# Norm statistics taken by token in thin matmuls, and three reorderings beside them

## The reference

```python
for l in range(2):                                   # first block, 272 tokens
    h = layer_norm(ALPHA*h + 0.5*swiglu(h, w_up1, w_down1))      # norm 0, 3
    h = layer_norm(ALPHA*h + hybrid_mixer(h, ...))               # norm 1, 4
    h = layer_norm(ALPHA*h + 0.5*swiglu(h, w_up2, w_down2))      # norm 2, 5
for l in range(2):                                   # second block, 256 tokens
    x = x + token_mixing(rmsnorm(x), ...)                        # rms 0, 2
    x = x + (swiglu_2, moe_swiglu)[l](rmsnorm(x))                # rms 1, 3
return rmsnorm(x)

def layer_norm(x, g, b): return (x - mean(x)) * rsqrt(mean((x - mean(x))**2) + eps) * g + b
def rmsnorm(x, g):       return x * rsqrt(mean(x*x) + eps) * g
```

## Time and profile before

| | us |
|---|---|
| three runs | 2813.75, 2813.24, 2811.03 |
| median | 2813.24 |
| span of the profiled execution, first to last instruction | 2809.8 |
| PE busy in it | 2745.6 (98%) |

### The profile page before, as it was taken

The page is one execution under the profiler, slowest core; times in us unless marked ns, Lnnn a source line. Parts: engine busy times, 40 slices in busy tenths (PEclk is TensorE's granted clock), DMA queues, the critical chain, the costliest instruction groups (busy, mean ns, idle before and its releaser), DMA issues.

```text
span 2809.8 us, 68032 instructions
## 1 busy us (share of the span) xinstructions
PE 2745.6 (98%) x28028; PEld 2292.6 (82%) x28028; DVE 1982.1 (71%) x1914; ACT 1608.7 (57%) x1723; POOL 700.7 (25%) x562
## 2 busy tenths in 40 slices
PE   9999999999999999999999999999999999999997
PEld 7887788888877888887888887888879788797794
DVE  5457575564576755666855566778899898998986
ACT  5445663354356554455643445657677776777765
POOL 4314022122122221120122011144234243242331
PEclk9999999999999999999999999999999999999999
DMA  9764367576643676553576663469999999999995
GB/s 240 171 199 124 91 194 195 169 191 176 188 134 106 180 206 178 157 181 121 179 189 180 200 187 124 151 240 365 383 386 383 387 387 378 394 383 382 388 384 223
DMA packets 657516, 665.64 MB, mean 237 GB/s; under 512 B 25302, under 2 KB 513116, under 8 KB 657276
## 3 DMA queue, kind: packets, MB, share of 16 engines
q1 hardware_dynamic: 655696, 659.75, 71.5%
q0 software_dynamic: 704, 0.59, 0.4%
q10 hardware_dynamic: 876, 1.79, 0.2%
HBM read 661.01 MB, written 1.05 MB: 236 GB/s over the span
## 4 chain that ended last, share of the span: by engine, by line
PE 91%; DVE 4%; ACT 2%; issue 1%; DVEq 1%; DMA 0%; POOLq 0%; ACTq 0%; SPq 0%; POOL 0%
PE ps L2084 23%; PE ps L2085 23%; PE ps L2086 23%; PE ps L2814 3%; PE ps L2813 3%; PE ps L2812 3%; PE ps L2127 1%; PE ps L2133 1%; PE ps L2128 1%; DVE w_lo L1258 1%; PE ps L2437 1%; PE ps L2417 1%; ACT w_hi L705 1%; PE ps L2747 1%; PE ps L2505 1%
## 5 line engine op out<-in xcount | busy, mean ns | idle before, releaser
L2084 PE MATMUL ps<-x_hi,w_hi 128*128 128x128 f16 (+2 forms) x5440 | 1229.5, 250 | 16.1 <-DVE prod L1273 5.4
L2085 PE MATMUL ps<-x_lo,w_hi 128*128 128x128 f16 (+2 forms) x5440 | 1229.2, 250 | 0.0
L2086 PE MATMUL ps<-x_hi,w_lo 128*128 128x128 f16 (+2 forms) x5440 | 1229.0, 250 | 0.0
L1258 DVE SCALAR_TENSOR_TENSOR w_lo<-w,w_hi 128x2048 f16<-128x2048 f32 (+4 forms) x338 | 692.5, 2059 | 309.4 <-ACT w_hi L705 307.6
L705 ACT ACTIVATE w_hi<-w 128x2048 f16<-128x2048 f32 (+4 forms) x338 | 560.9, 1669 | 83.7 <-PE ps L2086 70.4
L2084 PEld LDWEIGHTS ps<-x_hi,w_hi 128*128 128x128 f16 x5440 | 534.0, 98 | 71.2 <-issue 14.4
L2085 PEld LDWEIGHTS ps<-x_lo,w_hi 128*128 128x128 f16 x5440 | 533.8, 98 | 45.9
L2086 PEld LDWEIGHTS ps<-x_hi,w_lo 128*128 128x128 f16 x5440 | 533.9, 98 | 42.6
L1754 DVE SCALAR_TENSOR_TENSOR w_lo<-w,w_hi 128x2048 f16<-128x2048 f32 x224 | 532.8, 2406 | 40.9 <-ACT w_hi L1178 40.8
L1178 ACT ACTIVATE w_hi<-w 128x2048 f16<-128x2048 f32 x224 | 416.9, 1901 | 28.4 <-DMA w<-in_moe_w_gate 12.0
L2066 POOL CAST ff<-pb 128x512 f16<-128x512 f32 x56 | 137.6, 2458 | 568.5 <-DVE pb L1846 568.5
(11 more groups left out here) (390 smaller groups left out, 4302.3 us busy)
## 6 DMA issues: line engine op xcount, KB each, us to landing
w<-in_ffn_w_up SPq DMA_DIRECT2D x176, 512.0 KB, 5.0
w<-in_moe_w_gate SPq DMA_DIRECT2D x80, 1024.0 KB, 8.1
w<-in_moe_w_up SPq DMA_DIRECT2D x80, 1024.0 KB, 8.7
w<-in_moe_w_down SPq DMA_DIRECT2D x64, 1024.0 KB, 7.8
w<-in_w_in SPq DMA_DIRECT2D x112, 512.0 KB, 4.6
mix<-in_moe_w_down SPq DMA_DIRECT2D x48, 1024.0 KB, 8.0
w<-in_mix_w_in SPq DMA_DIRECT2D x64, 512.0 KB, 4.9
mix<-in_moe_w_gate SPq DMA_DIRECT2D x32, 1024.0 KB, 8.9
```

The costliest lines, as they stand in the source:

```text
L1258: vec.scalar_tensor_tensor(k.w_lo[:, s, 0:size], k.w32[:, s, 0:size], WS, k.w_hi[:, s, 0:size], ALU.mult, ALU.subtract).then_inc(k.parts_r ...
L2084: pe.matmul(acc, w_hi, x_hi, start=first, stop=False)
L2085: pe.matmul(acc, w_hi, x_lo, start=False, stop=False)
L2086: return pe.matmul(acc, w_lo, x_hi, start=False, stop=last)
```

## The change

1. Statistics by token. `windows(t)` cuts the tokens in windows of 128 (three for 272, the last one overlapping, two for 256). `turned_mean` makes the data the stationary operand and one column of `mean_w` the moving one: the result is one column of 128 tokens per window. The root and the reciprocal then work on 128x3 or 128x2 values, and `spread` brings 1/root back to all partitions with one matmul per window (stationary: the column broadcast to 128x128; moving: the identity). DVE's scaling `t` now reads it from PSUM.
2. The sums of the earlier chunks move into the last unit's chain (`within`, behind 8 of its 11 tiles in a down phase, behind 6 of 8 in `wo` and `wout`). The shift by the mean still needs the old wide form (`add_mean`), which stays beside the new one.
3. `keep_warm` becomes 4 idle matmuls ahead of the spread and 8 behind it.
4. The next phase's third unit is split ahead of the norm by ACT and DVE (`over_units_early`, and by hand in `wo` and `wout`). DVE's `up` takes the first product before it splits another unit.
5. ACT squares the latents ahead of `residual`, into `tmp`; the Silu table is loaded inside the norm (`silu=True`); layer 1's vectors are loaded (six DMAs on ACT's queue) ahead of norm 2's phase instead of behind it.

```diff
-KEEP_WARM = 13
+KEEP_WARM, KEEP_WARM_SPREAD = 4, 8
+SUMS_WITHIN, SUMS_WITHIN_WO = 8, 6
...
+def over_units_early(phase, q, split, take):
+    u0 = phase.units - AHEAD - 1
+    for u in range(phase.units):
+        for n in (u + AHEAD,) if u < u0 else (u + AHEAD, u + AHEAD + 1) if u == u0 else (u + AHEAD + 1,):
+            split(phase.first + n, q, phase.size if n < phase.units else UNIT)
+        take(u // SLOTS, u % SLOTS, phase.first + u % SLOTS, q + u // SLOTS)
...
 def layer_norm(n, ...):                                        # ACT
-        act.wait_ge(k.ln_rest, n + 1)
-        act.activation(k.tmp[:, 1, t], k.ps[:, 4, t], ACT.Square).then_inc(k.rest_squared, 1)
-        act.wait_ge(k.ln_spread, n + 1)
-        act.activation(k.std[:, 0, t], k.tmp[:, 1, t], ACT.Sqrt, bias=k.eps[:, 0:1]).then_inc(k.ln_std, 1)
-        split(following + 2, q, UNIT)
+        act.wait_ge(k.ln_var_out, n + 1)
+        act.activation(k.tok_std[:, 0:m], k.tok_var[:, 0:m], ACT.Sqrt, bias=k.eps[:, 0:1]).then_inc(k.ln_std, 1)
+        if silu:
+            act.activation(k.warm[:, :], k.eps[:, 0:1], ACT.Silu)
...
 def wo_norm(n, q):                                             # DVE
         add_pair(2, False)
+        split(g + 5, q, UNIT)
         vec.wait_ge(k.wo_half, n // 3 + 1)
         vec.tensor_tensor(k.h[:, 6, t], k.h[:, 6, t], k.ps[:, 0, t], ALU.add).then_inc(k.wo_half_out, 1)
-        split(g + 5, q, UNIT)
+        split(g + 6, q, UNIT)
...
 def layer_norm(n, g0, b0, last=False):                         # DVE
-        vec.tensor_tensor(k.tmp[:, 1, cols], k.ps[:, 5, cols], k.tmp[:, 1, cols], ALU.subtract).then_inc(k.ln_spread, 1)
-        u(0)
-        vec.wait_ge(k.ln_std, n + 1)
-        vec.reciprocal(k.rstd[:, 0, cols], k.std[:, 0, cols])
+        vec.tensor_tensor(k.tok_var[:, 0:m], k.ps[:, 5, 0:m], k.tok_less[:, 0:m], ALU.add).then_inc(k.ln_var_out, 1)
+        vec.wait_ge(k.ln_std, n + 1)
+        vec.reciprocal(k.tok_rstd[:, 0:m], k.tok_std[:, 0:m]).then_inc(k.ln_inverted, 1)
+        vec.wait_ge(k.ln_rest, n + 1)
+        u(0)
+        vec.wait_ge(k.ln_spread, n + 1)
...
+    def turned_mean(t, x, first=False, last=False, bank=5):    # PE
+        for m, (s, _) in enumerate(windows(t)):
+            a = pe.matmul(k.ps[:, bank, m:m + 1], x[:, s:s + P], k.mean_w[:, 0:1], ...)
+        return a
+    def spread(t, bank=5):
+        for m, (s, row) in enumerate(windows(t)):
+            a = pe.matmul(k.ps[:, bank, s + row:s + P], k.tok_rstd[:, m:m + 1].broadcast_to([P, P]), k.ident[:, row:P], start=True, stop=True)
+        return a
...
+        def within():                                          # down_norm, inside the last chain
+            pe.wait_ge(k.rest_summed, n + 1)
+            add_mean(n, k.prod[:, 1, :], first=True)
+            turned_mean(t, k.prod[:, 1, :], first=True, bank=6)
+            pe.wait_ge(k.squares_summed, n + 1)
+            turned_mean(t, k.prod[:, 0, :], first=True)
...
+                if cut:                                        # wo_norm, second half of unit 3
+                    chain(acc, g % SLOTS, tiles[:cut], k.x_hi[:, :, t], k.x_lo[:, :, t], last=False)
+                    pe.wait_ge(k.squares_summed, n + 1)
+                    turned_mean(t, k.prod[:, 0, :], first=True)
+                    for c in (4, 5):
+                        squared(n, c)
+                        turned_mean(t, k.sq[:, c, :])
+                    squared(n, 6)
+                    turned_mean(t, k.sq[:, 6, :])
+                    pe.wait_ge(k.rest_summed, n + 1)
+                    add_mean(n, k.prod[:, 1, :], first=True)
+                    turned_mean(t, k.prod[:, 1, :], first=True, bank=6)
...
+    def rms_begin(n):                                          # inside wout's and down's last chain
+        pe.wait_ge(k.squares_summed, 3 * DEPTH + n)
+        turned_mean(ALL2, k.prod[:, 0, :], first=True)
```

More of the change, by code:

```diff
@@ L176, with windows @@
 ALL1, ALL2 = slice(0, T1), slice(0, T2)
+def windows(t):
+    starts = [min(c, t.stop - P) for c in range(t.start, t.stop, P)]
+    return [(s, t.start + j * P - s) for j, s in enumerate(starts)]
 def live(l):
@@ L760, in take @@
                 square(n, c)
-        over_units_ahead(act, phase, q, split, take, loop=False)
+        over_units_early(phase, q, split, take)
     def wo_norm(n, l, q, vec0):
@@ L767, in wo_norm @@
         early_squares(n)
+        split(phase.first + phase.units + AHEAD, q, UNIT)
         act.wait_ge(k.vec_evac, vec0 + phase.base + 2 + 3)
@@ L807, in wout_squares @@
         for c in range(KC):
+            if c == 4 and l == 0:
+                split(phase.first + phase.units + AHEAD, 0, UNIT)
             if c == 6:
@@ L2199, in unit @@
                 pe.wait_ge(k.vec_evac, vec0 + (trip * 2 + j // 2) + (phase.base + 1))
-            chain(k.ps[:, 2 * (j // 2), t], g % SLOTS, [(c * P, P, second * half + c) for c in range(half)], a_hi[:, :, t], a_lo[:, :, t],
-                  first=not second, last=bool(second)).then_inc(k.unit_done, 1)
+            acc, s = k.ps[:, 2 * (j // 2), t], g % SLOTS
+            tiles = [(c * P, P, second * half + c) for c in range(half)]
+            if trip * SLOTS + j == 2 * KC - 1:
+                chain(acc, s, tiles[:SUMS_WITHIN], a_hi[:, :, t], a_lo[:, :, t], first=False, last=False)
+                within()
+                tiles = tiles[SUMS_WITHIN:]
+            chain(acc, s, tiles, a_hi[:, :, t], a_lo[:, :, t], first=not second, last=bool(second)).then_inc(k.unit_done, 1)
             if behind is not None:
                 behind(trip * SLOTS + j)
-        over_units(pe, phase, q, unit, loop=behind is None)
+        over_units(pe, phase, q, unit, loop=False)
     def wide(phase, q, evac, evac0, x_hi, x_lo, t, chunk=None, behind=None, late=False, turn=0):
@@ L2226, in add_mean, with spread_ln @@
         return pe.matmul(k.ps[:, 4, kept(n)], k.mean_w[:, :], x[:, kept(n)], start=first, stop=last)
-    def add_var(n, x, first=False, last=False):
-        return pe.matmul(k.ps[:, 5, kept(n)], k.mean_w[:, :], x[:, kept(n)], start=first, stop=last)
+    def turned_mean(t, x, first=False, last=False, bank=5):
+        for m, (s, _) in enumerate(windows(t)):
+            a = pe.matmul(k.ps[:, bank, m:m + 1], x[:, s:s + P], k.mean_w[:, 0:1], start=first and m == 0, stop=last and m == len(windows(t)) - 1)
+        return a
[3 more added lines that the diff above has]
+        return a
+    def spread_ln(n):
+        for _ in range(KEEP_WARM):
+            keep_warm()
+        pe.wait_ge(k.ln_inverted, n + 1)
+        spread(kept(n)).then_inc(k.ln_spread, 1)
+        for _ in range(KEEP_WARM_SPREAD):
+            keep_warm()
     def shift(n):
@@ L2238, in keep_warm @@
     def keep_warm():
-        for _ in range(KEEP_WARM):
-            pe.matmul(k.ps[:, 7, 0:P], k.mean_w[:, :], k.mean_w[:, :], start=True, stop=True)
+        pe.matmul(k.ps[:, 7, 0:P], k.mean_w[:, :], k.mean_w[:, :], start=True, stop=True)
     def down_norm(n, phase, vec0):
+        t = kept(n)
+        def within():
[4 more added lines that the diff above has]
+            turned_mean(t, k.prod[:, 0, :], first=True)
         def behind(u):
@@ L2308, in wout_norm @@
             for half in range(2):
-                a = chain(k.ps[:, 2 * (u % 2) + half, 0:T2], g % SLOTS, [(kc * 256 + half * P, P, kc) for kc in range(KC)], x_hi, x_lo)
+                acc, tiles = k.ps[:, 2 * (u % 2) + half, 0:T2], [(kc * 256 + half * P, P, kc) for kc in range(KC)]
+                cut = SUMS_WITHIN_WO if (u, half) == (3, 1) else 0
+                if cut:
+                    chain(acc, g % SLOTS, tiles[:cut], x_hi, x_lo, last=False)
+                    rms_begin(n)
+                    pe.wait_ge(k.rms_squared, n * KC + 7)
+                    turned_mean(ALL2, k.sq[:, 6, :])
+                a = chain(acc, g % SLOTS, tiles[cut:], x_hi, x_lo, first=not cut)
                 if (u, half) == (3, 0):
```

200 lines of the change are left out of this document (116 added, 84 removed).

## The result

Four runs of the changed kernel have a median of 2828.77 us (2824.48 to 2831.01), four of the kernel before 2813.49 us (2811.03 to 2813.78). The ratio is 1.0050, with a 95% interval from 1.0036 to 1.0065: slower by some 15 us, and 4 us above the upper end of the predicted range. The profiled run took 2831.01 us, its span is 2829.2 us (2809.8 before): 19.4 us more to find in the traces.

What follows compares the result with a forecast made beforehand. The prediction took PE, busy 98% of the span, to bound the kernel. Losses of 13.95 us less gains of 9.0 made +4.9 us on a 2809.8 us span, plus 3.4 us to the median: 2818.1 us, range 2805 to 2825.

Steps and rivals of the forecast that it cites:

- A thin pass takes 0.11 us: Sums with one moving column on PE: each pass costs 0.11 us, taken from bounds of half that and 0.11 us.
- cheap norm: Rival for all norms: one moving column costs half a pass and POOL wins the gaps; some 2806 us, chance 0.22.
- Norms 0 and 3: Norms over 272 tokens: +1.55 us each from chain sums and PE's queue, less 0.26 us at each opening.
- norm 2: Built like norms 0 and 3: +1.55 us, less 0.26 us at its opening.
- Norms 1 and 4: Norms behind `wo`: +2.2 us in norm 1; +0.4 us plus a 1.8 us wait for POOL in norm 4.
- The collision: DVE's moved splits stop POOL's additions, so PE waits 3 us in rms 1 (+2.9) and 1.8 us in norm 4.
- no collision: Rival in rms 1 and norm 4: POOL wins the gaps between DVE's splits; about 2813 us, chance 0.18.
- Gains: PE's waits removed: first low part 0.8, latents 4.3, third unit's low part 1.0, first products 2.9; 9.0 us.
- The clock: PE's granted clock may stay low in rms 0 under thin sums: +1.5 us taken, bounds -0.9 to +5 us.
- The sum: Whole kernel: losses 13.95 us, gains 9.0, net +4.9 us, giving 2818.1 us; chance 0.45.
- cold clock: Rival: rms 1's stop and rms 0's thin sums let the clock fall to half; +11 us, some 2824, chance 0.15.

Runs made afterwards that it cites:

- wide_column: The changed kernel with every thin sum moving all 128 columns of `mean_w` in place of one; 2819.05 us, ratio 1.0014.
- wide_late: The changed kernel with 128 moving columns in thin sums and the second low part of `wo` and `wout` split where it was before; 2812.15 us.
- stats_only: The kernel before with only the new statistics and their sums within the chain, everything else as before; 2836.4 us, ratio 1.0075.
- late_split: The changed kernel with the second low part of `wo` and `wout` split behind the last addition, as before; 2826.34 us, ratio 1.0043.
- latents_only: The kernel before with one edit, latents squared ahead of the residual into their own buffer; 2805.19 us, ratio 0.9970.

## Why the prediction was wrong

The forecast was 2818.1 us, the range 2805 to 2825, with 0.33 for slower by over 0.2%. Measured were 2828.8.

- **A thin pass takes 0.11 us: right.** Six passes take 0.69 us in norm 0. The *cheap norm* rival, with half of that, is refuted by the same row.
- **Norms 0 and 3: right; norm 2 at full clock only.** From the end of the chain to the opening norm 0 takes 5.8 us (202.14 to 207.92), predicted 6.0; the stages grew by 0.8 and 0.0 us where 1.6 and 0.3 were predicted. The stage of norm 2 grew by 2.1 us with 3.4 us at half clock, and by the predicted 0.6 us in wide_column without.
- **Norms 1 and 4: right at full clock, and only there.** From the end of unit 3's first half to the opening, wide_column takes 12.7 us in norm 1 and 12.0 in norm 4; predicted were 12.6 and 12.4 with the wait. The changed kernel takes 15.9 and 16.4.
- **The collision: the wait right, its consequence missed.** 2.98 us in rms 1 (predicted 3), 1.3 us in norm 4 (1.8). By the rule of the Trainium skill (SBUF — State Buffer, "SBUF: two separate sides") that whoever starts first has the port for a whole instruction, POOL might have been ahead. In the trace its addition that waited under the first split did end just behind it, while the second split, begun 0.3 us earlier, took 0.2 us longer than the 2.28 us of the earlier trace rows; so by these spans, which are rough for POOL, it got one addition in between, and that did not save PE the wait. The rival *no collision* falls. Missed was the half clock behind the stop: the stage is 2.8 us over its prediction, and wide_late shows 2.7 us to go with the stop.
- **Gains: right.** No wait for the squares or the third unit's low part, 0.27 us left of three product waits (0.3 predicted). Latents alone are worth 4.3 us by their two stages.
- **The clock: the step that failed.** The sum priced it in rms 0 alone, at +1.5 us, and the rival *cold clock* in rms 0 and rms 1, at 6.5 us beyond the sum (+11 in all) with a chance of 0.15. The argument against it was that once PE was kept busy the clock was back. But PE was kept busy there by 26 idle passes of 128 columns and by the float16 matmuls of the opening; the prediction took "busy" from the busy column, in which a thin pass counts like any other. The thin sums inside the chains (12 passes in norm 0, 30 in norm 1) were entered as 0.11 us a pass and no more. Beyond the sum stand 3.3 us in the stage of norm 1, 4.1 in that of norm 4 and 1.5 in that of norm 2. wide_column takes 9.7 us of the change's 15.3 away with nothing else changed, and lands at 2819 where the sum had 2818, in part because errors in its stages cancel.

So the sum was that of another kernel, the one with wide columns. The mechanism of the loss was named as a rival, in two of the places, and with 6.5 of the 10.7 us that were measured beyond the sum. In the profiled run its two places hold 3.5 us beyond the sum (2.8 in rms 1, 0.7 in the stage of rms 0); the stages of norms 1, 2 and 4, which it left out, hold 8.9.

What stays open: what picks the place. The clock falls at norm 2 and not at norms 0 and 3, which are built alike, at these two in stats_only, and at norm 0 in late_split with the very instructions of the changed kernel (norm 1 has 30 thin passes in its chain where these have 12, but that this makes it fall there every time was not tried). Each stretch is moreover read from one profiled run of a kernel. Open too is the rest of what latents_only gained.

## What to carry to other kernels

When work moves from wide matmuls to thin ones, price it twice: by PE's time a pass, and by what the granted clock does behind it, which is read in short stretches around the place and not in the busy share; the quickest test is to move more columns in the same instructions and look whether time comes back. An idle matmul that waits beside the data path may be holding the clock, so its width is part of the design. And of a change with several parts each one is worth its own run: here one edit of a few lines (latents_only) reached 2805 us by itself, and the rest hid it.

## What was not expected of the hardware

- Thirteen idle matmuls with 1 moving column take 2.96 us, with 128 columns 3.06 us; time at half clock is 99 us with the one and 34 us with the other over the program.
- At the lower clock eight float32 passes take 1.71 us instead of 0.89, and an opening's float16 matmuls start every 0.225 us instead of 0.115: the thin sums themselves can run at full clock and what follows them pays. The Trainium skill (TensorE: Matmul & The Clock Gate, "Why this matters for your kernels") warns of thin matmuls through their waits for DMA; here PE waits 0.53 us in norm 1 and for DVE, as it does with wide columns, and in that norm the clock falls only with thin ones.
- A stop of 3 us on POOL was followed by half clock even with wide sums (1418 to 1425 in wide_column), and one of 1.4 us was not (wide_late).
